# Expert products of the second pair in four column tiles of 32 slots, in a mixture-of-experts trunk on one Trainium2 core

## The reference, cut to what matters

```python
def run_block(args):            # one expert e on its tokens
    tok, e, wt = args
    h = x_pad[tok]              # gathered rows, width 1024
    y = (jax.nn.silu(h @ w_gate[e]) * (h @ w_up[e])) @ w_down[e]   # hidden width 256
    return y * wt[:, None]
```

## Time and profile before

| what | value |
|---|---|
| median of 3 runs | 1386.18 us |
| the profiled execution, its own time | 1388.24 us |
| its span, first to last instruction | 1386.5 us |
| mean granted TensorE clock | 0.988 of full speed |
| TensorE busy | 1347.8 us (97%) |
| VectorE, ScalarE busy | 564.2 us (41%), 357.3 us (26%) |
| chain of work that ended last | PE 95% |
| bytes read from memory | 466.76 MB, mean 338 GB/s |

### The profile page before, as it was taken

One profiled execution on the slowest core, in us unless ns is written; L12 is line 12 of the kernel. 1 busy time (PEld: TensorE's weight loads), 2 busy tenths in 40 slices (PEclk: granted clock), 3 DMA queues, 4 the chain that ended last, 5 costly groups with the idle time before them and its releaser, 6 DMA issues.

```text
span 1386.5 us, 19138 instructions
## 1 busy us (share of the span) xinstructions
PE 1347.8 (97%) x7240; PEld 800.3 (58%) x7240; DVE 564.2 (41%) x1123; ACT 357.3 (26%) x607; POOL 10.2 (1%) x24
## 2 busy tenths in 40 slices
PE   8999999999999999997999999999999999999996
PEld 8986445445445445436999997544454454454452
DVE  5756223322323322234577666423323233233234
ACT  4433111212211222113554442222122112122110
POOL 0000000000000000000000000000000000000000
PEclk9999999999999999998999999999999999999998
DMA  9765699999999999974444454479999999999991
GB/s 331 274 256 218 264 382 421 422 422 423 422 422 422 421 422 422 422 290 193 183 182 177 161 228 196 165 278 404 422 422 422 422 421 423 422 421 422 421 422 50
DMA packets 82767, 468.45 MB, mean 338 GB/s; under 512 B 7065, under 2 KB 19481, under 8 KB 32674
## 3 DMA queue, kind: packets, MB, share of 16 engines
q1 hardware_dynamic: 81296, 463.50, 82.4%
q10 hardware_dynamic: 1426, 4.33, 0.8%
HBM read 466.76 MB, written 1.05 MB: 337 GB/s over the span
## 4 chain that ended last, share of the span: by engine, by line
PE 95%; DVE 2%; issue 1%; ACT 1%; DMA 0%; POOL 0%; DVEq 0%; POOLq 0%; ACTq 0%
PE ps L578 32%; PE ps L600 17%; PE ps L678 10%; PE ps L536 9%; PE ps L556 9%; PE ps L690 6%; PE ps L712 5%; PE ps L761 2%; PE ps L586 1%; PE ps L615 1%; PE ps L522 1%; PE ps L543 1%; PE ps L745 1%; PE ps L754 1%; DVE acc L1088 0%
## 5 line engine op out<-in xcount | busy, mean ns | idle before, releaser
L578 PE MATMUL ps<-ring,xsT 128*64 128x512 f32 x2048 | 450.1, 592 | 1.7 <-DVE slot_tok L1064 1.7
L578 PEld LDWEIGHTS ps<-ring,xsT 128*64 128x64 f32 x2048 | 146.9, 137 | 293.0 <-issue 291.2
L600 PE MATMUL ps<-ring,hidT 128*64 128x512 f32 x1024 | 237.2, 606 | 2.3 <-ACT hidT L860 2.3
L1070 DVE SCALAR_TENSOR_TENSOR gated<-sig,slot_gate,ps 128x256 f32<-128x256 f32 x64 | 30.7, 480 | 364.7 <-ACT sig L856 364.7
L1002 DVE TENSOR_TENSOR ring_low<-ring,wh 128x1024 fp32r<-128x1024 f32 (+1 forms) x112 | 128.3, 1148 | 105.1 <-ACT wh L838 104.6
L1079 DVE TENSOR_TENSOR yl<-ps,yh 128x512 fp32r<-128x512 f32 x128 | 88.5, 691 | 169.2 <-ACT yh L865 169.2
L838 ACT CAST wh<-ring 128x1024 fp32r<-128x1024 f32 (+1 forms) x112 | 110.4, 988 | 156.5 <-PE ps L678 66.8
L600 PEld LDWEIGHTS ps<-ring,hidT 128*64 128x64 f32 x1024 | 68.6, 138 | 128.0 <-issue 124.4
L865 ACT CAST yh<-ps 128x512 fp32r<-128x512 f32 x128 | 74.9, 585 | 241.9 <-PE ps L600 241.9
L856 ACT ACTIVATE sig<-ps 128x256 f32<-128x256 f32 x64 | 24.6, 384 | 405.2 <-PE ps L578 405.2
L536 PE MATMUL ps<-sel,xh 128*128 128x256 f32 x512 | 127.8, 292 | 0.0
(11 more groups left out here) (150 smaller groups left out, 1270.9 us busy)
## 6 DMA issues: line engine op xcount, KB each, us to landing
ring<-in_w_gate SPq DMA_DIRECT2D x128, 1024.0 KB, 10.2
ring<-in_w_up SPq DMA_DIRECT2D x128, 1024.0 KB, 12.2
ring<-in_w_down SPq DMA_DIRECT2D x128, 1024.0 KB, 11.8
ring<-in_b_w_in SPq DMA_DIRECT2D x8, 3072.0 KB, 11.0
ring<-in_a_w_in SPq DMA_DIRECT2D x12, 1024.0 KB, 12.3
ring<-in_b_w_out SPq DMA_DIRECT2D x4, 3072.0 KB, 10.4
ring<-in_a_w_out SPq DMA_DIRECT2D x1, 3072.0 KB, 16.7
ring<-in_sh_gate SPq DMA_DIRECT2D x2, 1024.0 KB, 4.9
```

The costliest lines, as they stand in the source:

```text
L578: last = nc.tensor.matmul(ps[64 * half:64 * half + 64, p, :], xsT[:, c, (2 * p + half) * SLOTS:(2 * p + half + 1) * SLOTS], slot_gu(s)[:, ...
L600: last = nc.tensor.matmul(ps[64 * half:64 * half + 64, 4 + h, :], hidT[:, p, kk * P + 64 * half:kk * P + 64 * half + 64], slot_dn(s)[:, kk ...
```

## The change

`gate_up` and `down` loop over `TILES[p]` column tiles in place of two halves: the first pair (p = 0) runs as two tiles of 64 slots as before, the second pair (p = 1) as four tiles of 32 slots. Tiles 0 and 1 belong to the pair's first expert, tiles 2 and 3 to its second; each tile streams the whole 128 x 512 moving operand of its expert. The results are the same numbers at the same places. Waits and semaphores are as before. All later lines move down by one.

```diff
+TILES = [2, 4]
...
-                        for half in range(2):
-                            s = expert_slot(k, i, 2 * p + half)
-                            last = nc.tensor.matmul(ps[64 * half:64 * half + 64, p, :],
-                                                    xsT[:, c, (2 * p + half) * SLOTS:(2 * p + half + 1) * SLOTS],
+                        for tile in range(TILES[p]):
+                            s, w = expert_slot(k, i, 2 * p + tile * 2 // TILES[p]), P // TILES[p]
+                            last = nc.tensor.matmul(ps[w * tile:w * tile + w, p, :],
+                                                    xsT[:, c, p * P + w * tile:p * P + w * tile + w],
                                                     slot_gu(s)[:, c], start=(c == 0), stop=(c == KC - 1))
                     last.then_inc(k.gu_done, 1)
...
-                            for half in range(2):
-                                s = expert_slot(k, i, 2 * p + half)
-                                last = nc.tensor.matmul(ps[64 * half:64 * half + 64, 4 + h, :],
-                                                        hidT[:, p, kk * P + 64 * half:kk * P + 64 * half + 64],
+                            for tile in range(TILES[p]):
+                                s, w = expert_slot(k, i, 2 * p + tile * 2 // TILES[p]), P // TILES[p]
+                                last = nc.tensor.matmul(ps[w * tile:w * tile + w, 4 + h, :],
+                                                        hidT[:, p, kk * P + w * tile:kk * P + w * tile + w],
                                                         slot_dn(s)[:, kk, h * HALF:(h + 1) * HALF],
                                                         start=(kk == 0), stop=(kk == HC - 1))
                         last.then_inc(k.y_done, 1)
```

## The result

The changed kernel took 1400.04 us (median of 4 runs, 1396.63 to 1400.86) against 1386.82 (4 runs, 1386.15 to 1387.7): ratio 1.009, 95% interval 1.0072 to 1.0109, so 13 us slower. Forecast were 1394.2 us and slower; the time lies in the range, 6 us over the point. The profiled execution took 1400.39 us, its span is 1398.7.

The account below looks back on a forecast made before the run. The prediction took PE to bound the kernel, with the DMAs just keeping up. Border costs, shorter loads and later last tiles summed to 3.99 us a layer, 8.0 in all: 1386.18 + 8.0 = 1394.2 us, range 1385.5 to 1410.

Parts of the forecast that it names:

- PE sets the round and the DMAs just keep up: Expert rounds of 29.5 us: PE is busy throughout and sets the pace, with DMA share 0.99 to 1.01.
- 1,536 couples at nothing: Added weight loads with their matmuls, two more in each of 768 slots, hide beside the 0.43 us stream at no cost.
- The upper bound of 0.110 us a couple: Closest router spacing of load-and-matmul couples; four would take 0.44 to 0.46 us against a 0.43 us slot.
- The price of a border: Each switch of tile width between blocks costs a 0.09 us gap plus a bare first load, 0.025 or 0.05 us.
- The first rival: Switches between 64- and 32-wide tiles are free, the gap belonging to the tiled state: 1386.3 us, chance 0.15.
- Only two tiles at a time: Rival for 32-wide blocks: only two tiles overlap, a slot becomes two, +330 us to about 1724 us, chance 0.09.
- The sum: Width switches, load differences and later last tiles: 3.99 us per layer, 8.0 us over two layers.
- The time: Whole kernel: median 1386.18 + 8.0 = 1394.2 us, 0.6% slower.

Follow-up runs that it names:

- both pairs in four tiles: Both expert pairs run as four tiles of 32 slots, against the kernel before: 1387.27 us, ratio 0.9989; again 1388.04 us, 0.9996.
- both single kernels: Four tiles in gate_up(1) only, or in down(1) only, each against the kernel before: ratios 1.0028 and 1.0013.
- the alternating one: Kernel before, but gate_up(1)'s chunks take two tiles of 64 and four of 32 in turn: 1419.26 us, ratio 1.0223.
- the two kernels with regrouped chunks: Kernel before, but gate_up issues 2 or 8 chunks of one expert ahead of the other's: 1393.2 us and 1716.66 us.
- The second comparison: The changed kernel, unaltered, measured again in 6 runs against the kernel before: 1397.42 us, ratio 1.0062.
- down(1) alone: Only down(1) has four tiles, gate_up(1) keeps two, against the kernel before: 1390.39 us, ratio 1.0013.
- gate_up alone: Only gate_up(1) has four tiles, down(1) keeps two of 64, against the kernel before: 1393.02 us, ratio 1.0028.
- the mirror: First pair as four tiles of 32, second pair as two of 64, against the kernel before: 1396.88 us, ratio 1.0064.
- two chunks ahead: Kernel before, but gate_up issues two chunks of one expert, then two of the other: 1393.2 us in one run against 1389.17.
- eight chunks ahead: Kernel before, but gate_up issues all eight chunks of one expert, then all of the other: 1716.66 us.
- without the low part: Kernel before with the low part of the outputs left out of combine's sum: 1377.83 us in one run against 1389.17.

## Why the prediction was right, and where it was short

- *PE sets the round and the DMAs just keep up*: the first half is shown: PE's 0.3 us a round went to the time in full, and taking 57 us of work from it gave 11. The second half is not quite so. The DMAs' own round is 29.83 us against 29.54; they fall behind by 0.3 us a round, and the 16 rounds of a layer end before it shows.
- *1,536 couples at nothing*: shown by the block lengths with both pairs in four tiles (6.87) and by the four loads in 0.13 us. The upper bound of 0.110 us a couple did not come into play. Four couples in 0.43 us are 0.107 each, less than the router's 0.110, so that pace was not a limit of issue; opening a block, eight loads of 0.11 us lay within 0.16.
- *The price of a border*: right in mechanism and size. The gaps are 0.09 and 0.11 for the 0.09 put, the openings 0.03 and 0.05 as put; the changed kernel's blocks, both single kernels and the alternating one (27 forecast for the blocks counted, 29.8 found) agree. The first rival (no price between widths below 128) is refuted by these rows. Here the Trainium skill's rule (page TensorEngine Tiling (Array Packing), section Key Properties), that a change of mode drains the array and a change of tile doesn't, is in agreement with the rows of every kernel run here. They show a gap at each change of width and none between tiles of one width; the price is 0.12 to 0.15 us with the opening load. Whether the array drains in the gap no trace shows.
- *Only two tiles at a time*: refuted, by 226.4 us for twice the matmuls and by the two kernels with regrouped chunks. The strict order of starts that the Trainium skill states (page TensorE: Matmul & The Clock Gate, Part 3) does not hold between tiles here: three waiting couples are passed over. The prediction set the durations of line 578 beside an opening of line 600; the argument stands without them, since two that lie in 0.65 us did not run one behind the other.
- *The sum*: 8.0 forecast, 8.8 and 9.5 in the rounds of two profiles. The step that fell short is that no other block was given a change: gather was taken as it was, and it runs at two paces, which added 0.06 us to 12 and to 19 rounds, 0.7 and 1.1 us.
- *The time*: the first comparison gave 13.2, 5.2 above the sum. 3.4 us of span lay outside the rounds, at a lower granted clock. The prediction had no term for it. The second comparison, +8.5 us by its medians and 0.6%, is the 0.6% of the forecast, and at equal granted clock the difference was 7.6 to 9.8 us. That the second comparison came so near the point is partly luck: the slow gathers, about 1 us, had no term either.

What stays open: why gather takes one or the other pace, and whether the changed kernel meets the lower clock more often than the one before. Ten runs at 0.984 to 0.989 don't settle that, when the kernel with down(1) alone ran mostly at 0.990 and 0.991.

## What to carry to other kernels

Cutting a matmul into narrower column tiles was free here, where the narrow tiles together still fill the array, but each change of tile width cost a gap and a bare first load, 0.12 to 0.15 us. Choose one width for blocks that stand next to each other, and count the borders. Interleave the tiles finely: past a busy tile TensorE found the next one behind three waiting couples, and not behind four. Compare a small effect at equal granted clock, or in the rounds of a trace: with down(1) alone the medians showed 1.5 us of a cost of 4.3. And a DMA share of 1.0 next to a busy engine can mean that the loads are already losing ground, so look at how the time to landing moves through the layer.

## What the hardware showed that I had not expected

Gather has two paces. The same 16 matmuls of the same kernel, in the second layer of the repeated run, by the chain:

```profile
984.49 2.02 PE ps L537 x16
...
1014.31 2.08 PE ps L537 x16
```

The starts inside are 0.113 us apart in one round and 0.118 in the next, from the first matmul to the last, with the clock at 1.00 and the other engines at the same work. In the chain, of 28 gathers behind a gate_up(1), those of 2.08 or 2.09 us were 12 in the changed kernel, 19 in its repetition, 26 with gate_up alone and 24 in the mirror; none in the kernel before, with down alone, with alternating widths, with two chunks ahead, or in either run with both pairs; but 6 of 28 with eight chunks ahead, and without the low part 4 of the 14 that its chain shows, in kernels where no border between 64 and 32 exists. So it isn't the border as such.

Four plain float32 streams at once, two and two over the same 512 columns, ran at the pace of one (a slot of 0.43 us, as for the lone tile of the kernel with eight chunks ahead), with the DMAs moving 422 GB/s beside them.
